# Second attention of a two-block transformer kernel: two filling places of a step joined, the second head's transposes moved behind them

## The reference, cut to what matters

```python
def stick_breaking_attention(q, k, v):          # q, k, v: (1, 1024, 8, 64)
    for qb in range(s_len // Q_BLOCK):          # Q_BLOCK = 128, 8 blocks of queries
        z = jnp.einsum('bqhd,bkhd->bhqk', qi, kj) * scale
        log_rem = jnp.where(causal, jax.nn.log_sigmoid(-z), 0.0)
        suffix = lax.cumsum(log_rem, axis=3, reverse=True) - log_rem
        weights = jnp.where(causal, jnp.exp(log_sigmoid(z) + suffix), 0.0)
        o = jnp.einsum('bhqk,bkhd->bqhd', weights, vj)
```

## Time and profile before

| | |
|---|---|
| median of 3 runs | 2840.72 us (2840.35 to 2841.44) |
| profiled execution, span | 2840.6 us, with nothing counted around it |
| the four passes with what lies between them | 1600 to 1885 us, about 70.7 us a pass |
| PE busy / DVE / ACT / POOL, share of the span | 97% / 67% / 35% / 43% |

### The profile page before, as it was taken

How to read it: one execution, slowest core, us unless ns; L and a number is a source line. 1 busy time by engine, 2 the same in 40 slices (tenths; PEclk the granted TensorE clock), 3 DMA queues, 4 the chain that set the end, 5 groups by cost and what they waited for, 6 DMA issues and landing times.

```text
span 2840.6 us, 37829 instructions
## 1 busy us (share of the span) xinstructions
PE 2754.0 (97%) x15026; PEld 2216.1 (78%) x15026; DVE 1900.5 (67%) x2229; ACT 1007.7 (35%) x1482; POOL 1223.5 (43%) x720
## 2 busy tenths in 40 slices
PE   8999999998989999999999999999999999999999
PEld 6888777776768888888878666678778888888887
DVE  7777576667876677776768777755765555555555
ACT  5455433332432222222353455432332322232251
POOL 3111121112366676666765211222455554555553
PEclk9999999998999999999999999999999999999999
DMA  3111011002111111111112100012111111111111
GB/s 123 32 34 34 16 43 33 30 16 97 41 48 49 52 58 57 52 50 52 63 60 89 46 23 23 30 37 101 44 52 53 52 50 52 56 53 48 60 60 74
DMA packets 61641, 145.32 MB, mean 51 GB/s; under 512 B 7712, under 2 KB 8480, under 8 KB 61472
## 3 DMA queue, kind: packets, MB, share of 16 engines
q1 hardware_dynamic: 57152, 128.88, 14.3%
q10 hardware_dynamic: 4320, 14.09, 1.3%
HBM read 132.10 MB, written 8.49 MB: 49 GB/s over the span
## 4 chain that ended last, share of the span: by engine, by line
PE 82%; DVE 9%; issue 3%; POOL 3%; ACT 2%; DMA 0%; SPq 0%; ACTq 0%; DVEq 0%; POOLq 0%
PE ps L955 9%; PE ps L957 8%; PE ps L956 8%; PE ps L1077 8%; PE ps L1079 8%; PE ps L1078 8%; PE ps L1118 6%; PE ps L1120 6%; PE ps L1119 6%; PE ps L1242 2%; POOL ss L848 1%; PE ps L1473 1%; PE ps L1463 1%; PE ps L1487 1%; PE ps L1229 1%
## 5 line engine op out<-in xcount | busy, mean ns | idle before, releaser
L955 PE MATMUL ps<-a_hi,w_hi 128*128 128x512 f32 x1184 | 491.7, 415 | 11.8 <-POOL w_lo L825 10.6
L957 PE MATMUL ps<-a_hi,w_lo 128*128 128x512 f32 x1184 | 465.4, 393 | 0.0
L956 PE MATMUL ps<-a_lo,w_hi 128*128 128x512 f32 x1184 | 464.7, 392 | 0.0
L867 POOL TENSOR_TENSOR w_lo<-w_raw,w_hi 128x512 fp32r<-128x512 f32 x214 | 323.5, 1514 | 270.7 <-ACT w_hi L2409 270.6
L2084 DVE TENSOR_TENSOR x<-ps,x 128x512 f32<-128x512 f32 x432 | 295.1, 689 | 149.6 <-PE ps L1120 146.4
L820 POOL TENSOR_TENSOR w_hi<-w_raw,der 128x1024 fp32r<-128x1024 f32 (+1 forms) x57 | 105.7, 1854 | 654.4 <-PE ps L957 530.7
L2409 ACT ACTIVATE w_hi<-w_raw 128x512 fp32r<-128x512 f32 (+1 forms) x251 | 170.3, 680 | 543.3 <-PE ps L1120 238.1
L825 POOL TENSOR_TENSOR w_lo<-w_raw,w_hi 128x1024 fp32r<-128x1024 f32 (+1 forms) x74 | 193.3, 2613 | 279.4 <-ACT w_hi L2409 210.9
L955 PEld LDWEIGHTS ps<-a_hi,w_hi 128*128 128x128 f32 x1184 | 224.7, 190 | 61.1 <-issue 17.8
L957 PEld LDWEIGHTS ps<-a_hi,w_lo 128*128 128x128 f32 x1184 | 223.6, 189 | 49.1
L956 PEld LDWEIGHTS ps<-a_lo,w_hi 128*128 128x128 f32 x1184 | 224.8, 190 | 37.1 <-issue 0.2
(11 more groups left out here) (393 smaller groups left out, 6137.0 us busy)
## 6 DMA issues: line engine op xcount, KB each, us to landing
w_raw<-in_w_mix SPq DMA_DIRECT2D x54, 512.0 KB, 3.6
w_raw<-in_w_f SPq DMA_DIRECT2D x96, 256.0 KB, 2.6
w_raw<-in_w_gu SPq DMA_DIRECT2D x88, 256.0 KB, 2.6
w_raw<-in_w_ple SPq DMA_DIRECT2D x16, 512.0 KB, 3.6
chunk<-in_w_f SPq DMA_DIRECT2D x32, 256.0 KB, 3.1
chunk<-in_w_dn SPq DMA_DIRECT2D x22, 256.0 KB, 3.0
w_raw<-in_w_dn SPq DMA_DIRECT2D x22, 256.0 KB, 3.0
x<-in_x SPq DMA_DIRECT2D x8, 512.0 KB, 7.8
```

Source lines behind the costliest of these rows:

```text
L867: nc.gpsimd.tensor_tensor(ring(w_lo, r), src, ring(w_hi, r).bitcast(F32), ALU.subtract).then_inc(e_lo, 1)
L955: mm(ps[:, bank, :], wh, hi[:, k, cols], start=(k == 0), stop=False)
L956: mm(ps[:, bank, :], wh, lo[:, k, cols], start=False, stop=False)
L957: last = mm(ps[:, bank, :], wl, hi[:, k, cols], start=False, stop=(k == nk - 1))
```

## The change

Within a step the filling place that stood between the two heads' transposes and the one behind the second head's are joined into one place behind the first head's transposes. The second head's transposes come behind both, so they stand directly before the next step's logits. No instruction is added or removed, and nothing on the other engines is written in another order.

```diff
                     if n >= 2:
                         values(p, n - 2)
-                    for hh in range(2):
-                        if 1 <= n <= NSEG:
-                            turn(p, n - 1, hh)
-                        if n <= NSEG:
-                            fill(slots[2 * n + hh])
+                    if 1 <= n <= NSEG:
+                        turn(p, n - 1, 0)
+                    if n <= NSEG:
+                        fill(slots[2 * n])
+                        fill(slots[2 * n + 1])
+                    if 1 <= n <= NSEG:
+                        turn(p, n - 1, 1)
```

## The result

The changed kernel is slower by 0.2%: 2847.46 us median of 15 runs (2845.81 to 2850.64) against 2841.74 us of 15 runs of the kernel before taken beside it (2839.34 to 2843.92), ratio 1.0022 with a 95% interval of 1.0015 to 1.0028. The profiled execution has a span of 2846.9 us against 2840.6, that is +6.3. Forecast were +2.9 us and a range up to 2846.4, with 0.87 on a change of less than 0.2%. The sign is right, the size is half of what came.

The account below looks back on a forecast made before the run. PE's own stream was taken to bound the kernel, with DVE next. Passes 0 to 2 gave +1.7 us and pass 3 +1.25, together +2.9 on 2840.6: 2843.5 us, range 2840.4 to 2846.4.

Parts of the forecast that it names:

- term 3: Values newly wait for the second copy, mostly behind segments 9, 10 and 11 (0.92 each): +3.42 us a pass.
- the parts: Pass 3, last three steps: 0.92 of new wait less 0.17 saved by joining, 0.75 us a step.
- term 2: The wait for the first copy goes, 0.25 in five segments and 0.13 in segment 2: -1.38 us in passes 0 to 2.
- the clock stayed at 1.00: Rival: the clock falls at the ends of the passes, about 2 us each time, 8 us: 2851.5; chance 0.02.
- nothing behind the passes took the loss in: Behind the passes PE runs filling back to back, with nothing that could take a delay in.
- the price the trace lacked: Transposes followed directly by logits, 36 places: taken as 0, upper end 0.10, worth 1.2 us in 12 places.
- My first term: One filling place instead of two in each of 12 steps saves 0.17 a step: -2.04 us a pass.
- term 4: Before segment 7, passes 0 to 2: of PE's 1.16 gain 0.6 is passed on, giving back 0.56 a pass.
- DVE becomes the bound: Rival: late `sb` loses the 1.16 before segment 7, and a scan in pass 3: +7.1, 2847.7 us; chance 0.09.
- a real gain: Rival: first waits vanish and longer logits hide the values' wait: -8 us, 2835; chance 0.02.

Follow-up runs that it names:

- the light pair: POOL splits only 128 of 1024 columns per weight unit from the second gate projection on, in the changed kernel and the kernel before: 2836.6 and 2834.84 us.
- the split a place later: In passes 0 to 2 one `k_step` moved from place 13 to 14, in the kernel before and the changed kernel: 2836.99 and 2846.07 us.
- the light kernel: The changed kernel with POOL splitting only 128 of 1024 columns of each weight unit from the second gate projection on: 2836.6 us, one run.

## Why the prediction was wrong, step by step

**Right: the place of the loss.** The wait of the values for the second copy (term 3) came in 12 places, with 8.2 us of idle time in all. The values start 1.29 us after the second transposes; 1.33 was forecast. The idle time is less than the 11 to 14 us forecast, since the profile counts it from the modelled end of the transposes (0.60 after their start), and since the smaller waits that term 3 has behind segments 1, 3 and 5 (0.31, 0.28 and 0.07) came as 0.12, 0.13 and nothing: from logits to values it is 0.54 instead of 0.42 and 0.76 instead of 0.63. In pass 3 the last three steps cost 0.75 each, as the parts had said; in passes 0 to 2 0.36 (1.08 in three steps), where 0.92 - 0.25 - 0.17 = 0.50 was forecast: two of the three took 2.81 and 2.85 before the change, not the 2.75 of the last. The first copy's wait did go (term 2), the clock stayed at 1.00, and nothing behind the passes took the loss in.

**Wrong, the price the trace lacked: transposes to logits.** I took 0 for it, with 0.10 as the upper end. This is the timeline after, pass 0, the logits of segments 9 and 10:

```profile
1634.32 0.44 PE L1473 MATMUL ps<-ident,sw 128*128 128x128 f32 x2
1634.69 1.13 PE L1463 MATMUL ps<-sk_even 64*128 64x512 f32 x4
...
1641.12 0.60 PE L1473 MATMUL ps<-ident,sw 128*128 128x128 f32 x4
1641.65 1.13 PE L1463 MATMUL ps<-sk_even 64*128 64x512 f32 x4
```

Four transposes and the gap take 0.53 instead of 0.41. In pass 0 the distances are 0.20, 0.31, 0.42 and 0.53 behind one to four transposes, 0.11 to 0.12 more than the transposes need, and they are the same in all four passes, so it is no wait for another engine; only the two transposes above take 0.37, in passes 0 to 2. From the last matmul of a `k_step` to the logits it was 0.32, where the next `k_step` begins after 0.23: 0.09. So entering the logits costs 0.1 whatever stands before them. My first term booked this 0.09 as saved, a cost of "the change from filling", and booked nothing for entering from the transposes. It was the same cost and stayed. A joined step thus saves 0.03 at most where no wait is involved, as segments 0, 4 and 8 show in both pairs of traces (light and full), in place of 0.17. For the upper end I counted the price in 12 of the 36 places; all 36 have it. The nearest row was the wrong one: logits to values was chosen because both are plain float32, and what counted was what is entered. The rule of the Trainium skill that I had set aside ("TensorE: Matmul & The Clock Gate", Step-by-step: what each phase is for, and The mechanism), by which a weight load is pulled ahead of running matmuls only with other row groups or into the background buffer, would have put the sum 1.2 us higher, the right way. (It stands in these sections and not in the one on LDWEIGHTS that I named.) At the second pair of rows above, the weight load of the logits begins only with them, not ahead:

```profile
1641.65 0.30 PEld L1463 LDWEIGHTS ps<-sk_even 64*128 64x128 f32 x4 [0.17 <-issue]
```

The trace agrees that far. But one such load takes 0.18 and the gap is 0.12, so how the gap comes about stays open.

In numbers: up to segment 7 in passes 0 to 2 the gain is 0.55 instead of 1.16 (from the light pair, where no wait for `sw` lies in between), between segments 7 and 9 0.03 instead of 0.34, and in pass 3 up to segment 9 0.06 instead of 1.0. Together 3 x 0.61 + 3 x 0.31 + 0.94 = 3.7 us, of which term 4 would have given some back.

**Wrong, term 4: what becomes of the gain before segment 7.** I bounded what is lost by 0 and by the whole gain. The whole gain is no bound. I had seen that POOL would start 1.3 us sooner (it was 1.0, counted within the pass, as the gain before it was smaller) and that segment 6's `sw` would fall under the split, and priced that overlap as shared work, 0.8 us. But two short operations of DVE, worth 0.7 us, held each to the end of one half of the split, take 4.5, and the scans come after all of it. The two scans before the change had fared better: they took 5.57 in all, and POOL's second half was itself stretched, 3.18 instead of 2.39. So the place did not give back 0.56 of the gain: PE came 0.55 sooner to segment 6 and 0.45 later to segment 7, +1.00, the whole gain and 0.45 more. The runs with step 6 joined alone (+0.69), with a light split (-0.55) and with the split a place later show this as cause, not only as reading. My rival "DVE becomes the bound" named the place but the wrong path (`sb` behind the copy on ACT), let the gain before segment 7 be lost and no more, and had 0.09. That its total, 2847.7, lies 0.2 from the measured 2847.46 is luck: it counts one more scan in pass 3, and in pass 3 PE waited for no `sw`. (The rival "a real gain" has a slip: without 12 waits of 0.92 the sum is -8, which is 2832.6 and not 2835; it bears on nothing else.)

The page that bears on this is one I had not weighed: the Trainium skill, "SBUF — State Buffer", Who interferes with whom. It says that the port pair which VectorE shares with GpSimd is an exclusive lock, that a VectorE instruction with two inputs in SBUF contends with a GpSimd instruction that reads SBUF, that the order of issue decides who blocks, and that a VectorE instruction with at most one SBUF input (outside the 2-port modes) does not contend. The trace agrees: the mask takes 1.98 and the `sw` 2.57, and the eviction takes 0.68 with and without a split beside it. By that rule, and with the lengths of POOL's halves in this trace, my estimate for the two short products would have been 1.98 + 2.39 = 4.4 us, in place of 0.8. Measured are 4.55 (1.98 + 2.57).

The sum again with the measured sizes: passes 0 to 2 each +0.45 at segment 7, -0.03, +1.08, on average 1.49; pass 3 -0.06 and +2.26; 3 x 1.49 + 2.20 = 6.7.

What stays open is what the 0.1 before the logits is. It is larger only where the transposes before them had themselves waited: 0.37 behind the two that waited for `sw` in passes 0 to 2, with 0.31 in pass 3 and in the light kernel, where they did not; and 0.56 behind the four that waited for the copy in the runs with the split a place later, with 0.53 elsewhere. No run takes the gap apart.

## What to carry to other kernels

When a piece of covering work is moved from behind an instruction to before it, list for each step what then covers the wait that it had covered: here logits of 512 columns did, and at the end of each pass nothing did, at 0.36 to 0.75 us a step. Book a cost of changing from one kind of work to another on what is entered, not on what is left, before calling it saved. And where GpSimd's long operations are released by PE's work, look at which VectorE operation will meet them after the move: here a mask of 0.28 us that met one took 1.98.

## What the runs showed of the hardware

An operation of DVE with two inputs in SBUF that starts while a POOL operation of 128x1024 runs takes until POOL's ends, and then most of its own time: 1.98 us for a 128x128 product (0.28 alone), 2.57 for one of 128x256 (0.42 alone). The eviction from PSUM beside it keeps its 0.68 us: before the change it ran under the split at 1631.05, and after it at 1634.19 without. That the inputs decide fits the rule of the Trainium skill cited above ("SBUF — State Buffer", Who interferes with whom): the mask, the `sw` and the scans read two tensors in SBUF, the eviction reads one of its two from PSUM.

One held-up operation gets through between two of POOL's, and the longer it still has to run, the more the next one of POOL's is stretched over its 2.39 us. Behind the mask it is not stretched (the mask ends 0.15 after POOL's first half). Behind a `sw` of 384 columns (0.41 after; pass 3 of the changed kernel) it takes 2.58, behind one of 512 (0.55 after; the split a place later) 2.70, and behind a scan of 512 (1.08 after; before the change) 3.18. The other way round, POOL's first half took 2.28 instead of 1.93 in the run with the split a place later: it started at 1630.22, and a scan was still running until 1630.81.
